# Recurrence chunks on TensorE: the backward direction moved off the diagonal, and the products of the two directions alternated

## The reference

```python
def wkv7_scan(state0, p, d, reverse, emit):
    ...
    def step(S, inp):
        w_t, k_t, v_t, kk_t, a_t = inp[:5]
        sa = jnp.einsum('bhvk,bhk->bhv', S, kk_t)
        S = (S * w_t[:, :, None, :] - sa[..., None] * (kk_t * a_t)[:, :, None, :]
             + v_t[..., None] * k_t[:, :, None, :])
        return S, (jnp.einsum('bhvk,bhk->bhv', S, inp[5]) if emit else None)

    S, ys = lax.scan(step, state0, xs, reverse=reverse)

    # in odd_mixer
    s_fwd, yc_fwd = wkv7_scan(zero, cx, 0, False, need_ctx)
    s_bwd, yc_bwd = wkv7_scan(zero, cx, 1, True, need_ctx)
    _, y_fwd = wkv7_scan(s_fwd, lat, 0, False, True)
    _, y_bwd = wkv7_scan(s_bwd, lat, 1, True, True)
```

## Time and profile before

| | |
|---|---|
| median of 3 runs | 4833.1 us (4823.01 to 4834.37) |
| profiled execution | 4830.95 us |
| its span, first to last instruction | 4829.2 us |
| PE busy | 4169.2 us (86%) |
| DVE busy | 2249.1 us (47%) |
| ACT busy | 1458.7 us (30%) |
| POOL busy | 595.7 us (12%) |
| granted TensorE clock, mean over the span | 0.918 |
| instruction DMA queue q8, whole span | 264 packets, 4.33 MB |

### The profile page before, as it was taken

How to read it: one execution, slowest core, us unless ns; L and a number is a source line. 1 busy time by engine, 2 the same in 40 slices (tenths; PEclk the granted TensorE clock), 3 DMA queues, 4 the chain that set the end, 5 groups by cost and what they waited for, 6 DMA issues and landing times. The chain is left out here.

```text
span 4829.2 us, 85278 instructions
## 1 busy us (share of the span) xinstructions
PE 4169.2 (86%) x35880; PEld 3611.0 (75%) x35880; DVE 2249.1 (47%) x3566; ACT 1458.7 (30%) x2464; POOL 595.7 (12%) x749
## 2 busy tenths in 40 slices
PE   6786799999977668888998875799999995859999
PEld 5554588888964468886998765788888893548998
DVE  4454443334635644445444434443336854854444
ACT  2254321213234412113222333421123333633222
POOL 2010100001101332211000101100001102520000
PEclk8888899999988789998999887899999997869999
DMA  4446322222347831204332326322222344533332
GB/s 163 139 145 201 128 61 65 60 64 66 121 153 235 277 108 45 50 26 133 95 94 73 104 86 173 128 61 62 66 60 68 108 132 141 178 126 101 96 92 83
DMA packets 677460, 527.29 MB, mean 109 GB/s; under 512 B 124157, under 2 KB 600609, under 8 KB 677120
## 3 DMA queue, kind: packets, MB, share of 16 engines
q1 hardware_dynamic: 652800, 450.46, 31.1%
q0 software_dynamic: 24320, 71.89, 4.1%
HBM read 440.23 MB, written 82.01 MB: 108 GB/s over the span
## 5 line engine op out<-in xcount | busy, mean ns | idle before, releaser
L87 PE MATMUL acc<-h_hi,w_hi 128*128 128x258 f32 (+2 forms) x4416 | 1394.9, 316 | 45.0 <-DVE w_lo L478 33.0
L89 PE MATMUL acc<-h_hi,w_lo 128*128 128x258 f32 (+2 forms) x4416 | 1391.4, 315 | 0.0
L88 PE MATMUL acc<-h_lo,w_hi 128*128 128x258 f32 (+2 forms) x4416 | 1390.0, 315 | 0.0
L87 PEld LDWEIGHTS acc<-h_hi,w_hi 128*128 128x128 f32 x4416 | 833.2, 189 | 108.2 <-DVE w_lo L478 34.3
L88 PEld LDWEIGHTS acc<-h_lo,w_hi 128*128 128x128 f32 x4416 | 833.9, 189 | 57.8 <-issue 0.5
L89 PEld LDWEIGHTS acc<-h_hi,w_lo 128*128 128x128 f32 x4416 | 833.5, 189 | 56.1
L478 DVE TENSOR_TENSOR w_lo<-staged,w_hi 128x1024 fp32r<-128x1024 f32 (+1 forms) x414 | 488.4, 1219 | 137.1 <-ACT w_hi L356 134.0
L356 ACT CAST w_hi<-staged 128x1024 fp32r<-128x1024 f32 (+1 forms) x414 | 407.3, 1028 | 460.0 <-PE acc L89 363.6
L519 DVE COPY offset<-acc 128x2 f32<-128x2 f32 x276 | 43.7, 158 | 919.9 <-PE acc L89 916.8
L87 PE MATMUL acc<-hidden_hi,w_hi 128*128 128x512 f32 (+1 forms) x1200 | 420.2, 350 | 44.4 <-DVE hidden_lo L613 44.2
L88 PE MATMUL acc<-hidden_lo,w_hi 128*128 128x512 f32 (+1 forms) x1200 | 419.6, 350 | 0.0
(11 more groups left out here) (473 smaller groups left out, 6143.6 us busy)
## 6 DMA issues: line engine op xcount, KB each, us to landing
staged<-in_w_ffn_in SPq DMA_DIRECT2D x88, 512.0 KB, 4.5
staged<-in_ffn_w_in SPq DMA_DIRECT2D x88, 512.0 KB, 4.7
wmod<-in_w_mod SPq DMA_DIRECT2D x8, 3072.0 KB, 11.2
wmod<-in_mod_w SPq DMA_DIRECT2D x8, 3072.0 KB, 13.1
wmod<-in_mod_w SPq DMA_DIRECT2D x16, 1536.0 KB, 10.4
staged<-in_ssd_w_in SPq DMA_DIRECT2D x42, 512.0 KB, 4.5
rows<-acum SPq DMA_DIRECT2D x40, 512.0 KB, 5.3
wmod<-in_w_mod SPq DMA_DIRECT2D x8, 2048.0 KB, 8.1
```

The costliest lines, as they stand in the source:

```text
L87: nc.tensor.matmul(out, w[0], x[0], start=start, stop=False)
L88: nc.tensor.matmul(out, w[0], x[1], start=False, stop=False)
L89: return nc.tensor.matmul(out, w[1], x[0], start=False, stop=stop)
```

## The change

Direction 1's products are placed on the two other blocks of the array: the inputs keep their partitions and the output goes to the other half (`turned`), so a tile of direction 1 changes halves from product to product. Where a tile is needed in the half that it would not have, a product or a turn stays on the diagonal: in a level, direction 1's X product (into `six`) is turned and its Z product (into `one`) is not; the masks of level 1 need the beta product in both halves, so `betas_with` computes it once more into `big[1]`, from which DVE makes z, and `turn_values` puts one turn into `big[1]`, from which ACT copies.

Most groups now alternate the directions within one pass over h (`both`, `turn_both`), behind one wait for direction 1, which includes direction 0's. Within a level the forward X and Z products come first, as two groups, and then the backward X and Z alternated. The products with the state stay on the diagonal, all of `one` before `six`, and wait for two new semaphores. On DVE, masks of the next chunk come after all four adds of a level instead of between the directions. The removed lines below are cut where they stand in the printed functions above; the indent is reduced.

```diff
@@ -1994,120 +1994,169 @@
         pe.sem_inc(S["passed"], 1)
+    def product(out, lhs, rhs, h, c, turned, start, stop):
+        return nc.tensor.matmul(out[corners[1 - c if turned else c], h], lhs[corners[c], h], rhs[corners[c], h],
+                                start=start and (stop or h == 0), stop=stop and (start or h == H - 1))
     def each(out, lhs, rhs, name, start=True, stop=True):
         apart()
         for h in range(H):
-            for c in corners:
-                mm = nc.tensor.matmul(out[c, h], lhs[c, h], rhs[c, h], start=start and (stop or h == 0),
-                                      stop=stop and (start or h == H - 1))
+            for c in range(2):
+                mm = product(out, lhs, rhs, h, c, False, start, stop)
         if name:
             mm.then_inc(S[name], 1)
...
+    def both(out, lhs, rhs, name, start=True, stop=True):
+        apart()
+        for h in range(H):
+            for d in range(2):
+                for c in range(2):
+                    mm = product(out[d], lhs[d], rhs[d], h, c, d == 1, start, stop)
+                if name and h == H - 1:
+                    mm.then_inc(S[name], 1)
+    def pairs(ts):
+        return [t[:].rearrange("p h a c -> p h (a c)") for t in ts]
+    def side(ts, a):
+        return [t[:, :, a, :] for t in ts]
+    def turn(out, src, h, c, turned):
+        return nc.tensor.matmul(out[corners[1 - c if turned else c], h], src[corners[c], h], ident[corners[c], corners[c]],
+                                start=True, stop=True)
+    def turn_both(out, src, name):
+        apart()
+        for h in range(H):
+            for d in range(2):
+                for c in range(2):
+                    tr = turn(out[d], src[d], h, c, d == 1)
+                if name and h == H - 1:
+                    tr.then_inc(S[name], 1)
+    def keys_with(i, s, latent):
         arrived(pe, i, s, latent)
         if latent:
-            each(pair(front[d]), ka[s][d], pair(ar[s][d]), "kar")
+            both(pairs(front), ka[s], pairs(ar[s]), "kar")
         else:
...
+            both(side(front, 0), ka[s], side(ar[s], 0), "kar")
+    def betas_with(i, s, latent):
+        wait(pe, "mp_ready", i, 1)
+        apart()
+        wide = pairs(front), be[s], pairs(ar[s])
+        narrow = side(front, 0), be[s], side(ar[s], 0)
+        out, lhs, rhs = wide if latent else narrow
+        for h in range(H):
+            for d in range(2):
+                for c in range(2):
+                    mm = product(out[d], lhs[d], rhs[d], h, c, d == 1, True, True)
+                if h == H - 1 and d == 0:
+                    mm.then_inc(S["bar"], 1)
+        each(big[1][:, :, 0, :], be[s][1], ar[s][1][:, :, 0, :], "bar")
+    def turn_betas(i, s, latent):
+        wait(pe, "lt_ready", i, 1)
         if latent:
...
+            pe.wait_ge(S["q_ready"], 2 * i + (2 - 2 * CC))
+        turn_both(side(front, 0), be[s], None)
+        turn_both(side(front, 1), ka[s], "bk_t")
+    def turn_values(i, s, latent):
+        wait(pe, "kappa_c", i, 1)
+        wait(pe, "z1a", i, 1)
         apart()
         for h in range(H):
...
+            for c in range(2):
+                turn(front[0][:, :, 0, :], ar[s][0][:, :, 0, :], h, c, False)
+            for c in range(2):
+                turn(front[1][:, :, 1, :], vf[s][1], h, c, True)
+        for h in range(H):
+            for c in range(2):
+                tr = turn(front[0][:, :, 1, :], vf[s][0], h, c, False)
+        tr.then_inc(S["av_t"], 1)
+        for h in range(H):
+            for c in range(2):
+                tr = turn(big[1][:, :, 1, :], ar[s][1][:, :, 0, :], h, c, False)
+        tr.then_inc(S["av_t"], 1)
+    def turn_inverse(i, s):
+        wait(pe, "z1", i, 1)
+        wait(pe, "v_c", i, 1)
+        turn_both(side(front, 0), z[s], "x1_t")
     def core(i, s, latent, next_latent):
         ahead, s1 = has_next(i), 1 - s
+        wait(pe, "mp_ready", i, 1)
+        wait(pe, "v_c", i, 1)
+        if latent and not (type(i) is int and i <= CC):
+            pe.wait_ge(S["y_c"], 2 * i - 2 * CC)
+        both(six, side(mp[s], 0), vt[s], "mv_p")
+        for n in range(LEV):
+            if n == 0:
+                wait(pe, "x1", i, 1)
+                wait(pe, "levels", i, 1)
+                if not fresh(i):
+                    wait_last(pe, "state_c", i, 1)
+            else:
+                wait(pe, "x_c", i, 1, n - 1, LEV - 1)
+                wait(pe, "z_c", i, 1, n - 1, LEV)
+            both(one, [lev[s][d][n] for d in range(2)], x[s], "lx_p")
+            if ahead and n < 4:
+                (keys_with, betas_with, turn_betas, turn_values)[n](i + 1, s1, next_latent)
+            if n == 0:
+                wait(pe, "mv_c", i, 1)
+            wait(pe, "lx_c", i, 0, n, LEV)
+            if n < LEV - 1:
+                each(six[0], z[s][0], lx[0], "x_p")
+            each(one[0], lx[0], z[s][0], "z_p")
+            wait(pe, "lx_c", i, 1, n, LEV)
+            apart()
+            for h in range(H):
+                if n < LEV - 1:
+                    for c in range(2):
+                        mx = product(six[1], z[s][1], lx[1], h, c, True, True, True)
+                for c in range(2):
+                    mz = product(one[1], lx[1], z[s][1], h, c, False, True, True)
+            if n < LEV - 1:
+                mx.then_inc(S["x_p"], 1)
+            mz.then_inc(S["z_p"], 1)
+        wait(pe, "z_c", i, 1, LEV - 1, LEV)
+        if ahead:
+            wait(pe, "alpha_c", i + 1, 1)
+        both(pairs(big), z[s], pairs(am[s]), "au_p")
+        both(one, kt[s], vt[s], None, stop=False)
+        if latent:
+            both(six, vt[s], side(mp[s], 1), None, stop=False)
+        if ahead:
+            turn_inverse(i + 1, s1)
+        wait(pe, "au_c", i, 1)
+        if latent:
+            both(pairs(big), side(au, 0), pairs(bq[s]), "gf_p")
+        else:
+            both(side(big, 0), side(au, 0), side(bq[s], 0), "gf_p")
+        both(one, side(bq[s], 0), side(au, 1), "sums_p", start=False, stop=False)
+        if latent:
+            both(six, side(au, 1), side(bq[s], 1), "reads_p", start=False, stop=False)
+        wait(pe, "gf_c", i, 1)
+        if fresh(i):
+            pe.wait_ge(S["cleared"], 2)
+        wait(pe, "sums_p", i, 1)
+        if latent:
+            pe.wait_ge(S["reads_p"], 2 * i + (2 - 2 * CC))
         for d in range(2):
...
+            each(one[d], grow[d], state[d], None if latent else "core_p", start=False)
+        if latent:
             for d in range(2):
...
                 each(six[d], state[d], read[d], "core_p", start=False)
     for part in (keys_with, betas_with, turn_betas, turn_values):
...
+        part(0, 0, False)
+    turn_inverse(0, 0)
     chunks(pe, core)
 @block.vector
@@ -2131,7 +2180,8 @@
             V.tensor_tensor(bq[s][d][:, :, 1, :], front[d][:, :, 1, :], wide(masks[:, d, 2, :]), ALU.mult
                             ).then_inc(S["q_ready"], 1)
         wait(dve, "lt_ready", i, d)
-        V.tensor_tensor(z[s][d][:], lt[s][d][:], wide(masks[:, d, 3, :]), ALU.mult).then_inc(S["z1a"], 1)
+        from_lt = big[1][:, :, 0, :] if d else lt[s][d][:]
+        V.tensor_tensor(z[s][d][:], from_lt, wide(masks[:, d, 3, :]), ALU.mult).then_inc(S["z1a"], 1)
         wait(dve, "z1a", i, d)
         V.tensor_tensor(z[s][d][:], z[s][d][:], wide(eye), ALU.add).then_inc(S["z1"], 1)
@@ -2154,7 +2204,8 @@
                 if n:
                     wait(dve, "z_c", i, d, n - 1, LEV)
                 V.tensor_tensor(z[s][d][:], z[s][d][:], one[d][:], ALU.add).then_inc(S["z_c"], 1)
-                if ahead and n < 2:
+            if ahead and n < 2:
+                for d in range(2):
                     (mask_keys, mask_betas)[n](i + 1, s1, d, next_latent)
         for d in range(2):
             wait(dve, "au_p", i, d)
@@ -2203,7 +2254,7 @@
     def take_values(i, s, d):
         wait(act, "av_t", i, d)
-        A.copy(am[s][d][:, :, 0, :], front[d][:, :, 0, :]).then_inc(S["alpha_c"], 1)
+        A.copy(am[s][d][:, :, 0, :], big[1][:, :, 1, :] if d else front[d][:, :, 0, :]).then_inc(S["alpha_c"], 1)
         A.copy(vt[s][d][:], front[d][:, :, 1, :]).then_inc(S["v_c"], 1)
     def core(i, s, latent, next_latent):
```

More of the change, by code:

```diff
@@ L2009, in keys_with @@
-                def keys_with(i, s, d, latent):
+                def both(out, lhs, rhs, name, start=True, stop=True):
[8 more added lines that the diff above has]
+                    return [t[:].rearrange("p h a c -> p h (a c)") for t in ts]
@@ L2023, in turn @@
-                def turn(out, src, name):
+                        both(side(front, 0), ka[s], side(ar[s], 0), "kar")
[12 more added lines that the diff above has]
+                    each(big[1][:, :, 0, :], be[s][1], ar[s][1][:, :, 0, :], "bar")
@@ L2025, in turn @@
+                def turn_betas(i, s, latent):
+                    wait(pe, "lt_ready", i, 1)
+                    if latent:
+                        pe.wait_ge(S["q_ready"], 2 * i + (2 - 2 * CC))
```

(55 more changed lines are left out.)

36 lines of the change are left out of this document (1 added, 35 removed).

## The result

The changed kernel takes 4856.7 us (median of 7 runs, 4845.1 to 4860.8), beside 4832.0 us for the kernel before (7 runs, 4816.8 to 4834.8): ratio 1.0055, 95% interval 1.0039 to 1.0071. It is slower by 0.55%, 25 us. Forecast was 4824, range 4790 to 4856.

A forecast was written before the change was run, and what follows sets the result against it. PE in the recurrence was taken as bound by instruction packets (4.18 us per 123 passes), waits and some slow clock; seven latent, four context and the last chunk save 9.4 us: 4821.5, median 2 above, 4824; own range 4811 to 4837, wider 4790 to 4856.

The forecast's parts named there:

- (1) Four tiles at once: Alternating both directions over four array corners: a 32-pass group takes 0.47 us, a wide one 0.87.
- D: Rival, chance 0.08: corners sharing rows or columns do not overlap, alternated groups cost 0.93 us, kernel 4875 us.
- E: Rival, chance 0.10: 20.7 ns a pass, 0.19 us more on some fourteen groups, kernel 4833 us.
- (2) Instructions: PE's instruction supply: 16 passes added a chunk, packets stay at 90, 33.2 us a latent chunk, 29.9 a context one.
- B: Rival, chance 0.06: instruction packets come as fast as PE asks, chunks take 31.4 and 27.2 us, kernel 4772 us.
- (3) The walk: PE's groups and merged waits summed level by level: 31.4 us a latent chunk, 27.2 a context one.
- (4) Both limits together: Instruction blocks of 123 passes at 4.18 us laid on the chunk's groups and waits: latent 34.8 us, context 30.8.
- (5) The clock: A tenth of the recurrence stage at clock 0.50 adds 1.3 us: latent chunk 36.0 us, context 31.8.
- case C: Rival, chance 0.14: clock falls at level 2's wait and stays; break-even 16% of the stage, at 40% 4865 us.
- case A: Rival, chance 0.17: the clock holds, as idles of 2.6 us are shorter than 3.60; gain 22 us, kernel 4811.

## Why the prediction was wrong

The direction was wrong and the time lay just outside the range. By its own steps:

**(1) Four tiles at once** was right: 0.47 for an alternated group and 0.87 for a wide one were taken, 0.48 and 0.89 measured. D and E are out. By the rule of the Trainium skill, "TensorE: Matmul & The Clock Gate", "Wait — 56ns, not 53.3ns?", starts are never closer than about 25 ns; 32 passes in 0.48 us are 15 ns, so the trace disagrees.

**(2) Instructions** was right in number: 90 packets. That B would hold is refuted by 55 us of idle on issue. Its bound of 3.75 us a block was read as two blocks' worth from rows that hold 224 passes, 1.8 blocks, in 6.84 us; scaled to a block that gives the same 3.75. The Trainium skill's "Runtime: NRT & Kernel Launch", Instruction fetch mechanics, has the crossing mostly hidden; here the stalls are an eighth of the stage.

**(3) The walk** was nearly right. The new wait in level 2 was put at 2.6 us and is 2.30; the chunk without its stalls was put at 31.4 and is 32.8 in mean in the run with the clock nearly held, its added matmuls included. But it costed one thing at nothing that isn't: the semaphore instruction behind each wait, 0.15 us, was inside its "back to PE".

**(4) Both limits together** is the first step that failed. It laid blocks of 123 passes at 4.18 us over the walk and let all but two of the eight hide their waits in the time for the packet, which left 3.4 us of stalls on 31.4. Measured are 5.5 in a latent chunk of the changed kernel and 4.8 on 32.8 with the clock nearly held. There the chunk is 37.6 instead of 34.8, 2.8 us more, half of it stalls and half the rest: about 20 of the 25 us that are missing. The premise that failed is that "the next block is asked for when the last is entered". In the rows it was read from, PE resumes at 2001.90 and the next packet starts at 2003.6. After the change it starts 1.35 us after PE resumes where no wait for DVE or ACT lies between, and 2.8 us after where one does (medians). A wait early in a block therefore delays the next block too, and the two limits add up where the prediction overlapped them.

**(5) The clock** is the second, and as large. Taken was a tenth of the stage at 0.50; it was 22%, above the 16% that case C named as the point from which it decides. C's sum at the measured share of latent chunks (clock 0.88, so 24%) gives 34.8 + 0.24 x 13.2 = 38.0; measured are (287.8 - 48.4) / 6 = 39.9 beside the jump, and the rest falls to step (4). C itself had said about two falls a chunk, and 4865; it was given a chance of 0.14, which was too low. The reason held against C, that the clock rises again under steady work, was true but beside the point: it falls again in nearly every chunk. The one fall of the earlier trace rows had followed an idle of 3.60 us, and case A leaned on its being longer than what the change brings; after the change a fall followed one of 2.30. In the run with those waits removed it still fell to 0.90, with waits for DVE of up to 1.1 us and idles on issue of up to 2.5 outside the loop's jump. Which pattern makes it fall is not settled; that it does, and what it costs, is.

The Trainium skill, "TensorE: Matmul & The Clock Gate", Part 1: The HAM clock gate, puts the penalty of the ramp to full clock under 1% of a typical kernel's span. Here the slow stretches come back chunk after chunk, and still the runs agree for the kernel as a whole: 24 us of 4857. But that is 5% of the stage, and it decides the sign.

The bill in the profile, against the forecast: six latent chunks 39.9 instead of 36.0, 23 us; the jump's chunk 48.4 instead of 36.0 + 6.3, 6; context 130.5 instead of 127.2, 3; the last 31.9 instead of 27.9, 4; the prologue, first matmul to first mv on PE's timelines, 15.6 instead of 12.5, 3, said to be under 1 and run wholly at 0.50. Together 39.9: the 9.4 of forecast gain and the 30.5 by which prologue and chunks grew. The rest of the span was 5 us shorter than before, which nothing in the change touches.

That the order costs more than placement returns is measured on both sides: order alone +51 us, placement within it -25, order repaired with the same placement -31. What stays open is how the last 25 us divide: the traces put some 10 of them in stalls for instructions and 8, by estimate, in what was left of the slow clock, and no experiment separates the two.

## What to carry to other kernels

When engine time shrinks, ask what the engine lives on in the gaps: PE here halved its group times and got idle instead, first on instructions, then on waits that used to be covered, and then its clock went with its activity. A faster array pays only if the waits are reordered with it: put independent groups behind the products whose results DVE needs, not before them, and look at the granted clock after every change that makes PE less busy. Two limits read from one trace should be added before they are overlapped, unless a row shows them hiding each other. Here the rows showed the next packet starting 1.7 us after PE had resumed, which was enough to ask whether a wait in between would push it back.

## What the runs showed of the hardware

**A matmul that feeds nothing can pay.** Six extra matmuls of 128x128 by 256 columns a chunk made the changed kernel 24 us faster (9 either way), and three the reordered one 11 us (ratios 0.9991 and 0.9968).

**Half the columns, more time.** At a granted clock of 0.50 a 32-pass group of 64x64 products takes 0.88 us with 32 columns and 0.87 with 64. With every 64x64 product at half its columns the clock was at 0.58 in the mean, and the kernel slower by 1.4% than with all of them.

**The next block of instructions is fetched from within the last one.** After the change 44 of 45 idles on issue end 2.2 to 3.0 us after an instruction packet starts. The packet after it starts 1.35 us after PE resumes where no wait for another engine lies between, and 2.8 us after, up to 5.5, where one does.

**A semaphore instruction on PE costs 0.15 to 0.17 us where it follows a wait**, three more of them 0.51 us on each of 44 waits; where PE has matmuls in its queue, 17 fewer a chunk were worth 5 us in all, within the uncertainty.
